# RWKV-7 chunks with stacked operands: one Gram product a head, joint transposes, and solved rows and values in one 128-row buffer

## What is computed

```
def step(S, inp):
    r_t, w_t, k_t, v_t, kk_t, a_t = inp
    sa = jnp.einsum('bhvk,bhk->bhv', S, -kk_t)
    S = (S * w_t[:, :, None, :]
         + sa[..., None] * (kk_t * a_t)[:, :, None, :]
         + v_t[..., None] * k_t[:, :, None, :])
    o_t = jnp.einsum('bhvk,bhk->bhv', S, r_t)
    return S, o_t
```

## Time and profile before

| | us |
|---|---|
| runs, median (lowest to highest of 3) | 2788.75 (2785.66 to 2795.35) |
| the profiled execution | 2785.38 |
| span of the profile (first to last instruction) | 2783.8 |
| PE busy | 2581.4 (93%), 18133 matmuls |
| PE weight loads | 2110.5 (76%) |
| DVE busy | 992.0 (36%) |
| ACT busy | 653.2 (23%) |
| mean granted clock of TensorE | 0.959 |

### The profile page before, as it was taken

How to read it: one execution, slowest core, us unless ns; L and a number is a source line. 1 busy time by engine, 2 the same in 40 slices (tenths; PEclk the granted TensorE clock), 3 DMA queues, 4 the chain that set the end, 5 groups by cost and what they waited for, 6 DMA issues and landing times.

```text
span 2783.8 us, 43617 instructions
## 1 busy us (share of the span) xinstructions
PE 2581.4 (93%) x18133; PEld 2110.5 (76%) x18133; DVE 992.0 (36%) x1760; ACT 653.2 (23%) x1065; POOL 19.1 (1%) x26
## 2 busy tenths in 40 slices
PE   5999999899999999999999999709699999999997
PEld 3677767667676767767676767609599999999996
DVE  1122212245363636454453636282322222222212
ACT  2221312221222222232312222221333311111111
POOL 0000000000000000000000000000000000000000
PEclk9999999899999999999999999659899999999999
DMA  4011101100000000000000000022011111111112
GB/s 148 31 49 45 50 28 48 49 1 32 2 32 1 15 18 2 32 2 32 2 32 2 32 1 8 26 88 78 5 48 45 45 45 46 45 47 51 39 46 81
DMA packets 23545, 99.55 MB, mean 36 GB/s; under 512 B 5040, under 2 KB 5232, under 8 KB 19456
## 3 DMA queue, kind: packets, MB, share of 16 engines
q1 hardware_dynamic: 21792, 88.45, 9.4%
q0 software_dynamic: 1632, 9.21, 0.9%
HBM read 86.31 MB, written 11.34 MB: 35 GB/s over the span
## 4 chain that ended last, share of the span: by engine, by line
PE 87%; DVE 8%; issue 2%; ACT 1%; DMA 0%; SPq 0%; DVEq 0%; ACTq 0%
PE banks L545 87%; ACT arena L968 1%; DVE arena L1564 1%; DVE arena L1572 1%; DVE arena L1573 1%; DMA arena<-in_consts 0%; DVE arena L1555 0%; DVE arena L1554 0%; DVE arena L1575 0%; DVE arena L1566 0%; DVE arena L1319 0%; DVE arena L1729 0%; ACT L968 0%; DVE merged_low L1654 0%; DVE arena L1759 0%
## 5 line engine op out<-in xcount | busy, mean ns | idle before, releaser
L545 PE MATMUL banks<-arena 64*64 64x64 f32 (+9 forms) x12770 | 1735.7, 311 | 157.5 <-DVE arena L1682 58.4
L545 PEld LDWEIGHTS banks<-arena 64*64 64x64 f32 (+2 forms) x12770 | 1264.5, 167 | 626.1 <-issue 299.2
L545 PE MATMUL banks<-merged_high,gate_up_high 128*128 128x344 f32 x1056 | 338.6, 321 | 23.6 <-DVE gate_up_low L1713 23.6
L545 PE MATMUL banks<-x_low,gate_up_high 128*128 128x344 f32 x1056 | 337.8, 320 | 0.0
L545 PE MATMUL banks<-merged_high,gate_up_low 128*128 128x344 f32 x1056 | 337.8, 320 | 0.0
L968 ACT ACTIVATE arena<-arena 128x64 f32<-128x64 f32 (+5 forms) x285 | 170.7, 616 | 377.9 <-DVE arena L1499 253.8
L1713 DVE TENSOR_TENSOR gate_up_low<-arena,gate_up_high 128x1024 fp32r<-128x1024 f32 (+1 forms) x76 | 82.3, 1084 | 432.8 <-ACT gate_up_high L1237 432.8
L545 PEld LDWEIGHTS banks<-merged_high,gate_up_high 128*128 128x128 f32 x1056 | 198.8, 188 | 24.1 <-issue 24.1
L545 PEld LDWEIGHTS banks<-merged_high,gate_up_low 128*128 128x128 f32 x1056 | 198.9, 188 | 0.0
L545 PEld LDWEIGHTS banks<-x_low,gate_up_high 128*128 128x128 f32 x1056 | 198.9, 188 | 0.0
L545 PE MATMUL banks<-hidden_high,gate_up_high 128*128 128x344 f32 x528 | 169.3, 321 | 0.0
(11 more groups left out here) (149 smaller groups left out, 1414.8 us busy)
## 6 DMA issues: line engine op xcount, KB each, us to landing
arena<-in_w_gu SPq DMA_DIRECT2D x44, 512.0 KB, 3.6
arena<-in_w_pair SPq DMA_DIRECT2D x8, 2112.0 KB, 8.1
arena<-in_w_gla SPq DMA_DIRECT2D x12, 1024.0 KB, 4.9
arena<-in_xT SPq DMA_DIRECT2D x16, 516.0 KB, 6.5
arena<-in_w_d SPq DMA_DIRECT2D x16, 384.0 KB, 3.1
arena<-in_w_d SPq DMA_DIRECT2D x16, 320.0 KB, 2.8
out_yT<-arena SPq DMA_DIRECT2D x8, 516.0 KB, 3.0
arena<-in_gla_s POOLq DMA_DIRECT2D x4, 1024.0 KB, 5.1
```

The lines of the kernel that those rows point to most:

```text
L545: return nc.tensor.matmul(out, lhsT, rhs, start=start, stop=stop)
```

## The change

- **One Gram product a head.** `BK` holds both decayed keys of a chunk side by side (64 + 64 columns, head 0 as b, k and head 1 as k, b). For each chunk and head one product of 64 rows by 128 weight columns replaces two of 64 by 64; the two heads go to two banks, and two quarters are in flight (banks 3 to 6). DVE masks a head's quarter with one operation into `G`; `Y` is taken from `G`, half by half, and the block sums are made in two halves. The block matrix `GTB` is now copied from `G` by ACT, ahead of `norm_root`.
- **Joint transposes.** `BK` of a chunk (128 x 128) is turned in one transpose; 16 replace 64 products. ACT copies four groups into `BKT`. V is still turned by products, into the other head's rows of `UV`, with two half copies a group.
- **Values and solved rows in one buffer.** `UV[:, c, e, :]` has the 64 values and the 64 solved rows of a head on 128 partitions. The state update is one product of 128 rows a head, the output two (`UV`·`G` over 128 rows, `S`·`AR` over 64). The solved rows are written by two DVE operations, one a head, with a change of sign.
- **The values' part of the right-hand side ahead.** `values_of(c + 1)` is made after stage 1 of chunk c, from `G` and the values in the other head's rows (two products of 64 x 64, banks 7 and 6); ACT copies it to `AV`; DVE adds it when it takes the right-hand side out.
- **Scans in pieces**, one a chunk, over a row of ones: 16 of 64 columns in four steps in a pair, 8 of 128 columns in a GLA head. The constant rows `C_RR` and `C_RG` go, and the gains move into the constants' transfer (3496 columns of constants instead of 4235, one transfer less). Buffers move in the arena.

The core of the diff:

On PE, in `chunk_step`:

```diff
+                def values_of(n):
+                    if n == 0:
+                        gate(inv_yr, i * 7 + 6)
+                    if n == 9:
+                        gate(o_ready, i * 2 + 1)
+                    for e, r in enumerate(HALVES):
+                        q = HALVES[1 - e]
+                        last = mm(bank[AVBANK(n)][r, 0:HD], G[q, n, e, 0, :], UV[q, n, e, :], True, True)
+                    last.then_inc(av_done, 1)
+
                 if stage == 0:
+                    if c == 0:
+                        values_of(0)
                     gate(s_ready, i * (NC + 1) + (c + 1))
-                    for r in HALVES:
-                        mm(bank[3][r, 0:HD], AK[r, c, 0, :], VTT[r, c, :], True, False)
-                        last = mm(bank[3][r, 0:HD], AR[r, c, 0, :], S[r, :], False, True)
+                    for e, r in enumerate(HALVES):
+                        last = mm(bank[3][r, 0:HD], AR[r, c, 0, :], S[r, :], True, True)
                     last.then_inc(rhs_done, 1)
                 if stage == 1:
...
                     mm(bank[4][:, 0:HD], YB[c // 8][:, c % 8, :], RH, True, True).then_inc(u_done, 1)
+                    if c + 1 < NC:
+                        values_of(c + 1)
                 if stage == 2:
-                    gate(u_ready, i * NC + (c + 1))
-                    for r in HALVES:
-                        mm(bank[5][r, 0:HD], KTT[r, c, :], VTT[r, c, :], True, False)
-                        last = mm(bank[5][r, 0:HD], BTT[r, c, :], U[r, :], False, True)
+                    gate(u_ready, i * (2 * NC) + 2 * (c + 1))
+                    for e, r in enumerate(HALVES):
+                        last = mm(bank[5][r, 0:HD], BKT[:, c, r], UV[:, c, e, :], True, True)
                     last.then_inc(s_done, 1)
...
-                    for r in HALVES:
-                        mm(ob[r, cols], VTT[r, c, :], AK[r, c, 1, :], True, False)
-                        mm(ob[r, cols], S[r, :], AR[r, c, 1, :], False, False)
-                        last = mm(ob[r, cols], U[r, :], GT[r, c, :], False, True)
+                    for e, r in enumerate(HALVES):
+                        mm(ob[r, cols], UV[:, c, e, :], G[:, c, e, 1, :], True, False)
+                        last = mm(ob[r, cols], S[r, :], AR[r, c, 1, :], False, True)
                     last.then_inc(o_done, 1)
```

On PE, in `chunk_products`:

```diff
+                    if m < 4:
+                        for c in range(4):
+                            last = nc.tensor.transpose(to[:, c * 128:(c + 1) * 128],
+                                                       BK[:, 4 * m + c, :, :].rearrange("p a t -> p (a t)"), IDF)
+                    else:
                         for c in range(8):
...
+                            for e, r in enumerate(HALVES):
+                                last = mm(to[HALVES[1 - e], c * CR:(c + 1) * CR], V[r, t0:t0 + CR], IDS[r, :], True, True)
...
                 for q in range(4):
+                    if q == 1:
+                        gate(tr_ready, i * 8 + 6)
+                    if q >= 2:
+                        gate(gram_ready, i * 8 + (2 * q - 2))
+                    for c in range(4):
+                        for e, r in enumerate(HALVES):
+                            last = mm(bank[3 + 2 * (q % 2) + e][:, c * 128:(c + 1) * 128],
+                                      BK[r, 4 * q + c, :, :].rearrange("p a t -> p (a t)"),
+                                      AR[r, 4 * q + c, :, :].rearrange("p a t -> p (a t)"), True, True)
+                            if c == 3:
+                                last.then_inc(gram_done, 1)
```

On ACT, in `chunk_side` and `second_phase`:

```diff
+                def value_product(n):
+                    act.wait_ge(av_done, i * NC + (n + 1))
+                    nc.scalar.copy(AV[n % 2], bank[AVBANK(n)][:, 0:HD]).then_inc(av_ready, 1)
+
+                if s == 0:
+                    value_product(0)
+                if s % 3 == 1 and c + 1 < NC:
+                    value_product(c + 1)
...
                 if previous:
                     norm_square(i, job + 1)
+                for hf in range(2):
+                    act.wait_ge(gram_ready, i * 8 + (4 * hf + 4))
+                    for e in range(2):
+                        r = slice(64 * e, 64 * e + 64)
+                        nc.scalar.copy(GTB[hf][r, :, r], G[r, 8 * hf:8 * hf + 8, e, 0, :]).then_inc(gtb_ready, 1)
+                if previous:
                     norm_root(i, job + 2)
```

On DVE, in `first_phase`, `chunk_side` and `second_phase`:

```diff
-                    V_.tensor_tensor_scan(B, CON[:, C_RR:C_RR + T], B, 0.0, ALU.mult, ALU.add).then_inc(ldr, 1)
+                def decay_sums(part):
+                    for c in range(4 * part, 4 * part + 4):
+                        cs = slice(CR * c, CR * c + CR)
+                        V_.tensor_tensor_scan(B[:, cs], ONES[:, 0:CR], B[:, cs], 0.0, ALU.mult, ALU.add).then_inc(ldr, 1)
...
-                    V_.tensor_tensor(KE, KP[:, 0:T], EM[:, 0:T], ALU.mult).then_inc(gram_in, 1)
-                    V_.tensor_tensor(BE, BE, EM[:, 0:T], ALU.mult).then_inc(gram_in, 1)
+                    for e in range(2):
+                        r = slice(64 * e, 64 * e + 64)
+                        for src, at_ in ((KP, 1 - e), (A, e)):
+                            V_.tensor_tensor(BK[r, :, at_, :], src[r, 0:T].rearrange("p (c t) -> p c t", t=CR),
+                                             EM[r, 0:T].rearrange("p (c t) -> p c t", t=CR), ALU.mult).then_inc(gram_in, 1)
...
-                    V_.tensor_copy(RH, bank[3][:, 0:HD]).then_inc(rhs_ready, 1)
+                    dve.wait_ge(av_ready, i * NC + (c + 1))
+                    V_.tensor_tensor(RH, bank[3][:, 0:HD], AV[c % 2], ALU.add).then_inc(rhs_ready, 1)
...
-                    V_.tensor_copy(U, bank[4][:, 0:HD]).then_inc(u_ready, 1)
+                    for e in range(2):
+                        r = slice(64 * e, 64 * e + 64)
+                        V_.tensor_scalar(UV[r, c, e, :], bank[4][r, 0:HD], -1.0, None, ALU.mult).then_inc(u_ready, 1)
...
+                    for e in range(2):
+                        dve.wait_ge(gram_done, i * 8 + (2 * q + e + 1))
+                        V_.tensor_tensor(G[:, 4 * q:4 * q + 4, e, :, :].rearrange("p c a t -> p c (a t)"),
+                                         bank[3 + 2 * (q % 2) + e].rearrange("p (c t) -> p c t", t=2 * CR),
+                                         over(CON[:, C_MK:C_MK + 2 * CR], 4), ALU.mult).then_inc(gram_ready, 1)
+                    if q % 2:
...
+                            ins = V_.tensor_tensor(Y[r, cs, :], G[r, cs, e, 0, :], over(CON[r, C_S8:C_S8 + CR], 8), ALU.mult)
...
+                        st(V_.tensor_reduce(N8[:, cs, :], Y[:, cs, :].rearrange("p c (b t) -> p c t b", t=SUB), AX_X, ALU.add))
```

More of the change, by code:

```diff
@@ L239, in hybrid_step @@
         RH = at(take(HD), HD)
-        U = at(take(HD), HD)
+        AV = [at(take(HD), HD) for _ in range(2)]
         DC = at(take(NC), NC)
         LNP = at(take(2), 2)
-        pair_end = o
         assert max(gla_end, pair_end) <= 53200, (gla_end, pair_end)
+        assert o <= 22720 and A0 + SUB * NC * 2 <= t0ofs + 1 + XC
         Q_R, Q_KP, Q_V, Q_KK, Q_KA, Q_W = range(6)
@@ L270, in hybrid_step @@
         WOL = [at(f_ + 2048 + 1024 * j, KT, 128) for j in range(2)]
-        F_SQ = [at(A0 + TS * kt, TS) for kt in range(KT)]
+        F_SQ = [at(HB + TS * kt, TS) for kt in range(KT)]
         F_RS = at(f_ + 4096, TS)
@@ L785, in chunk_products @@
                 job = base(i) + 6
-                gate(gram_in, i * 4 + 2)
-                for n_, (src, idn) in enumerate(((KE, IDS), (BE, NIDS), (V, IDS))):
-                    if n_ == 2:
+                gate(gram_in, i * 6 + 4)
+                for m in range(6):
+                    if m == 4:
                         for b in range(3):
@@ new lines, in chunk_products @@
+                    last.then_inc(tr_done, 1)
+                    if m < 3:
+                        projection(i, SPREAD + 2 * m)
+                        projection(i, SPREAD + 2 * m + 1)
+                gate(gram_in, i * 6 + 6)
+                for q in range(4):
+                    if q == 1:
[9 more added lines that the diff above has]
+                                last.then_inc(gram_done, 1)
```

198 lines of the change are left out of this document (90 added, 108 removed).

## The result

The changed kernel took 2929.4 us (median of four runs, 2922.55 to 2946.03) beside 2788.9 for the kernel before on the same chip: a ratio of 1.051, 95% interval 1.0462 to 1.0557. It is slower, as forecast, but by 140 us and not by 82; 2929 lies above the range. One run of experiment 11 took 3937 us and one of experiment 8 took 2921.5; both are left out of the ratios there, as runs in a slow state. The profiled execution took 2922.55 us with a span of 2921.0, 137.2 more than the span of the earlier trace rows.

The account below looks back on a forecast made before the run. PE's instruction stream was taken to bound the kernel. Chunk phases +72, last chunk phase +8, products phases -7, clock +10 and start -1 made +82 on 2785.4: 2867, range 2786 to 2895.

Parts of the forecast that it names:

- Stage 2 at 1.18: Chunk's stage 2, 20 loads to 12: alternating shapes drain PE at each inner change, 1.18 a chunk, +4.5 a phase.
- Rivals 1 and 2: Stage 2: inner changes free, outputs queue (0.65; 2792; 10%), or stacked products run in full pairs (0.50; 2773; 7%).
- The value product at +0.41: Value product in a visit of its own after stage 1 pays the shape change anew: +0.41 a chunk, +6.3 a phase.
- Stage 0, the scan and the keys: Per chunk phase: stage 0's 8 loads to 4, -1.9; PE's scan wait gone, -1.2; decayed keys' longer block, +2.3.
- rival 1: Stage 2's inner changes are free and outputs queue as today: 0.65 a chunk, 2792 in all; chance 10%.
- The last chunk phase at +8: Last chunk phase, without projections: PE's change doubles at half clock (0.32), second copy unhidden (0.2); +0.5 x 16 = +8.
- Clock in chunk phases: +10 (ends -10, +25): Chunk phases: further half-clock stretches from the keys' wait and more shape changes, at most 5.1 each; +10 together.
- two to four more: Half-clock stretches of 10.2 us expected in chunk phases beyond the three of the kernel before.
- the first queues behind block copies of the phase before: +0.3: Start of a chunk phase: the first value product's copy on ACT waits behind block copies (0.62 each), +0.3 a phase.
- Products phase at -7: Eight products phases: transposes -2.2, Gram +1.6 with a PE wait of 4.9 and half clock; -7 together (ends -34, +5).
- rival 3: Products phase: clock falls where the transposes stand, some 5 us at 1.2 GHz, +5 x 8, 2907 in all; chance 5%.
- The 11.4 for VectorE's work: Products phase, first mask to end of block rows on DVE: 13.5 before, 11.4 after, so -2.0.
- Start at -1: Program start: a sixth less of constants to transfer, -1 (0 to -2).

Follow-up runs that it names:

- experiment 11: Kernel before, plus two 64-column products (four loads) behind stage 1 of each chunk but the last, into columns nothing reads: 2819.6 us, ratio 1.0095.
- experiment 8: Kernel of experiments 7, with eight of the twelve gate matmuls ahead of the spreading product instead of four: 2808.9 us, ratio 1.0047.
- experiment 4: Changed kernel, with stage 2 issuing both heads' 128-row output products first, then both 64-row ones: 2864.8 us, ratio 1.0255.
- experiment 5: Changed kernel, with the four operations that write the decayed keys spread one each over four slots: 2907.8 us, ratio 1.0407.
- experiment 6: Changed kernel with the order of experiment 4, and the next chunk's value product moved to the end of stage 2: 2819.9 us, ratio 1.0093.
- experiment 14: Kernel before, with one more block copy (0.62 us) on ScalarE ahead of the last of the inversion's block copies: 2810.1 us, ratio 1.006.
- experiment 2: Changed kernel, VectorE's loop kept but placed about 100 instructions further down by 200 waits ahead of it: 2918.9 us, ratio 1.0451.
- experiment 1: Changed kernel, with VectorE's pair loop written out so that its program has no jump back: 2922.5 us, ratio 1.046.
- experiment 10: Kernel of experiments 7 without the placing of VectorE's loop: 2782.9 us, ratio 0.9977.
- experiment 13: Kernel of experiments 7, with the first value product copied ahead of the inversion's last two block copies: 2758.7 us, ratio 0.9882.
- experiment 9: Kernel of experiments 7, with six of the twelve gate matmuls ahead of the spreading product instead of four: 2899.3 us, ratio 1.042.
- experiments 7: Changed kernel with output order, values behind output, loop placed, norm's root ahead of Gram block copies, and keys spread, together: 2766.2 us, ratio 0.9897.

## Why the prediction was right or wrong

- **Stage 2 at 1.18: right**, 1.15. The three inner changes do drain PE, as the sentence from the Trainium skill (TensorEngine Tiling (Array Packing), Key Properties) had it, and each of the two that experiment 4 took away was worth 0.25. Rivals 1 and 2 are out for the order that the change chose. The 0.65 of rival 1 is what another order of the same products takes, with one change left; 0.50 was not seen.
- **The value product at +0.41: right for a chunk**, 0.40 by itself in experiment 11; over that run's whole phase it is 0.35. **Stage 0, the scan and the keys: right**: 0.26; no wait at the scan; a wait of 2.1 at the keys. Without the clock a chunk phase costs 16 x 0.53 + 2.1 (the last step, 6.9 for 4.3, less the 0.53) - 1.2 = +9.4; the forecast had 10.3. (The -1.2 for the scan is the forecast's: that chunk lies in the half-clock stretch, and no run shows it alone.)
- **The last chunk phase at +8**: 3.81 - 3.47 = 0.34 a chunk, +5.4. The sign is right; which of its two parts was too large is not settled.
- **"Clock in chunk phases: +10 (ends -10, +25)": wrong, this is the step that failed.** The chunk phases cost 99.0, and 7 x 9.4 = 66 of that is work and waits; the other 33 go with the clock. That is by subtraction; an estimate from the trace agrees with most of it: three stretches of 10.24 cost the kernel before 3.3 each (78.7 for 75.4), and at that rate the 106 us of stretches at the starts here cost 34, 24 more than before. I counted "two to four more" stretches of 10 us, with the wait at the keys and the changes of shape as their cause. There are fourteen: seven at the start, 13.65 to 20.48 long, and seven of 6.83 behind the keys. The keys' wait is a cause (experiment 5). A visit's changes of shape don't do it alone (experiment 11), though the stretch got shorter when the visit went (experiment 6). PE's wait at the start of the phase bears on it (experiment 14), and I had that wait on the page: "the first queues behind block copies of the phase before: +0.3" priced the 0.3 and not the clock behind it.
- **Products phase at -7: wrong**, +11.7. By the forecast's terms the stage up to `L8` was to gain 2.2 + 2.0 = 4.2 a pair, and the stage up to `Y` to lose 1.6 + 2.0 = 3.6 in seven pairs. The second came about as forecast, +3.1: the wait of 5 and the clock at 0.50. The first failed: pair 0, at full clock, gained 4.1, and the others 0.7 to 1.7, because the stretch behind the keys' wait reached the transposes. That is the place of rival 3, at some half of its price and with another cause: not the transposes but the wait ahead of them (experiment 5). (The 11.4 for VectorE's work is some 11.0 by its own terms; the trace has 12.0, from 1301.78 to 1313.75.)
- **A term that was missing: the jump of VectorE's loop**, +14.8. I counted what each added instruction costs where it runs, and did not ask where the loop lies, whose body grew from 282 to 334 instructions. It is not a plain 14.8 here: taken away, it gave 4 us of span in experiment 2 and none in experiment 1 (11 and 7 by the medians), since the half-clock stretch grew; with the other waits gone it was worth 16.7 (experiment 10).
- **Start at -1: wrong**, +5.3 with the first pair's projections, where the keys' longer block stands on the path too (4.7 us for 2.3).

In sum: 66 + 33 (chunk phases) + 11.7 + 14.8 + 5.3 + 6.3 = 137.1, against 72 + 10 - 7 + 0 - 1 + 8 = 82. The work of the chunk phases was forecast to within 6 us; 23 of the miss is the clock in chunk phases, 19 the products phase, mostly the clock again, and 15 the jump. The side was right for the reason that the forecast gave, the changes of shape in a chunk; the size was not, for the clock.

What stays open: what brings the stretches at the starts. They got shorter with PE's wait but did not go (experiment 13). With the wait unchanged and an inversion that begins at half clock, six of seven were gone in experiment 8, and six of seven were there in experiment 9. So something in the inversion ahead bears on them too. That was not tried by itself.

## What to carry to other kernels

Where a chunk mixes tile shapes, order its products so that equal shapes stand together: the same twelve loads took 1.15 or 0.65 us, and four loads 0.40 in a visit of their own against 0.12 behind others of their shape. Price each new wait of PE twice, once for its length and once for the half-clock stretch that may follow, and read the granted clock of the stages around it after each edit: a fall can move. When a loop's body grows, count its instructions and where they lie in the program.

## What the runs showed that I had not expected

- **The clock can take back what a shorter wait gains.** With the jump's 2.45 us taken out, pairs stayed at 170.3 to 171.0 us: PE came to the chunk phase sooner, and the half-clock stretch was 17.07 instead of 13.65 in five of seven.
- **A busy stage can stay at half clock.** In experiment 9 the inversion, PE busy in all of it, ran 68 us at 0.50 and took 73.5 instead of 40.8; with eight gate products ahead of the spreading product the same stage came back to 1.00 after 17 us in six pairs of seven. Four, six or eight of them made 2766, 2899 or 2809 us, with PE's waits there at 4.06; 2.90 and 1.80; 1.74 and 2.97. The time does not follow the longest wait.
- **The same wait of PE can stand ahead of 10 us at half clock or of none**: 1.09 at the start of a chunk phase in experiments 7 and 8.
- **The jump back of a loop on VectorE costs 2.75 to 2.96 us or 0.29 to 0.34**, by where the loop lies: from about instruction 250 to 583 of the program it is dear, from 350 to 683 and (before) from 229 to 510 it is not.
- **Of two changes of shape that go, each is worth 0.25 us**: 0.15 for the longer way from the last load of one shape to the first of the next (0.20 for 0.05), and the rest because a head's product that stands alone doesn't run beside the other head's.
